# Four output projections as three fp32r products of high and low parts

## What is computed

```
first_block, for each of 2 layers:
    x = x + 0.5 * rms_norm(swiglu(rms_norm(x)))                         # ffn1
    merged = sum over b in conv, nsa, mem of sigmoid(gate_b) * (y_b @ w_branch_b)  # token mixer
    x = x + rms_norm(merged @ w_mix_out)                                # [256,1024] @ [1024,1024]
    x = x + 0.5 * rms_norm(swiglu(rms_norm(x)))                         # ffn2
second_block:
    even layer: concat(ssd scan [256,1024], dilated attention [256,512])
    x = x + concat @ even_w_out                                         # [256,1536] @ [1536,1024]
    odd layer: block attention over 16 heads, gated by silu
    x = x + heads @ odd_w_out                                           # [256,1024] @ [1024,1024]
```

## Time and profile before

| | us |
|---|---|
| median of 3 runs | 1951.61 |
| lowest, highest | 1950.76, 1953.88 |
| profiled execution | 1953.57 |
| its span | 1951.8 |
| PE busy | 1837.4 (94%) |
| DVE busy | 1038.3 (53%) |
| ACT busy | 912.4 (47%) |
| POOL busy | 228.2 (12%) |

### The profile page before, as it was taken

One profiled execution on the slowest core, in us unless ns is written; L12 is line 12 of the kernel. 1 busy time (PEld: TensorE's weight loads), 2 busy tenths in 40 slices (PEclk: granted clock), 3 DMA queues, 4 the chain that ended last, 5 costly groups with the idle time before them and its releaser, 6 DMA issues. The chain is left out here.

```text
span 1951.8 us, 29977 instructions
## 1 busy us (share of the span) xinstructions
PE 1837.4 (94%) x11744; PEld 1576.7 (81%) x11744; DVE 1038.3 (53%) x1976; ACT 912.4 (47%) x1397; POOL 228.2 (12%) x115
## 2 busy tenths in 40 slices
PE   6999999989999989999999989899979899998989
PEld 6999798878599979999897877799969777764875
DVE  7555462346355556554552354555557783552762
ACT  5444433884343444443435882444365444332463
POOL 1000001536200010000004544100010000001000
PEclk9999999999999989999999999999989889799999
DMA  7445456324354444445445323554435333103521
GB/s 286 176 183 193 172 194 245 144 98 159 143 184 176 189 172 160 175 182 194 173 176 236 140 98 136 199 194 177 180 127 194 130 129 130 65 1 129 193 98 55
DMA packets 29900, 311.58 MB, mean 160 GB/s; under 512 B 3312, under 2 KB 3696, under 8 KB 4848
## 3 DMA queue, kind: packets, MB, share of 16 engines
q1 hardware_dynamic: 28944, 307.16, 42.3%
q0 software_dynamic: 864, 3.15, 0.5%
HBM read 309.24 MB, written 1.05 MB: 159 GB/s over the span
## 5 line engine op out<-in xcount | busy, mean ns | idle before, releaser
L428 ACT ACTIVATE region_r<-ring 128x1024 fp32r<-128x1024 f32 x451 | 471.6, 1054 | 422.4 <-PE psum L778 361.5
L778 PE MATMUL psum<-hH,region_r 128*128 128x256 f32 x2240 | 557.0, 287 | 21.5 <-DVE small L2072 8.7
L434 DVE TENSOR_TENSOR ring_r<-ring,region_r 128x1024 fp32r<-128x1024 f32 x398 | 474.8, 1222 | 183.9 <-ACT region_r L428 168.5
L778 PE MATMUL psum<-xs_r,region_r 128*128 128x256 f32 x2240 | 550.6, 284 | 0.0
L778 PEld LDWEIGHTS psum<-hH,region_r 128*128 128x128 f32 x2240 | 425.4, 190 | 36.7 <-DVE small L2072 12.7
L778 PEld LDWEIGHTS psum<-xs_r,region_r 128*128 128x128 f32 x2240 | 425.4, 190 | 4.8 <-issue 0.5
L778 PE MATMUL psum<-hH,ring_r 128*128 128x256 f32 x2336 | 324.7, 281 | 0.0
L778 PEld LDWEIGHTS psum<-hH,ring_r 128*128 128x128 f32 x2336 | 298.3, 189 | 0.0
L434 POOL TENSOR_TENSOR ring_r<-ring,region_r 128x1024 fp32r<-128x1024 f32 x53 | 116.9, 2216 | 1071.2 <-ACT region_r L428 1071.2
L778 PE MATMUL psum<-region_r 128*128 128x512 f32 x704 | 235.0, 395 | 2.1 <-DVE region_r L2019 2.1
L778 PE MATMUL psum<-region_r,hH 128*128 128x512 f32 (+3 forms) x544 | 178.3, 363 | 18.1 <-DVE xs_r L440 6.2
(11 more groups left out here) (213 smaller groups left out, 1895.2 us busy)
## 6 DMA issues: line engine op xcount, KB each, us to landing
ring<-in_weights SPq DMA_DIRECT2D x192, 1536.0 KB, 6.4
gpost<-in_posts POOLq DMA_DIRECT2D x6, 512.0 KB, 5.0
cst<-in_const SPq DMA_DIRECT2D x1, 1198.0 KB, 23.1
xs<-in_mem SPq DMA_DIRECT2D x1, 1024.0 KB, 5.5
x<-in_x SPq DMA_DIRECT2D x1, 1024.0 KB, 7.6
out<-x SPq DMA_DIRECT2D x2, 512.0 KB, 2.6
pars<-in_par SPq DMA_DIRECT2D x1, 368.0 KB, 8.0
p<-in_par SPq DMA_DIRECT2D x1, 206.0 KB, 24.3
```

The source lines that it names most:

```text
L428: eng.activation(unit.high, unit.raw, ACT.Copy).then_inc(h_ready, 1)
L434: eng.tensor_tensor(unit.low, unit.raw, unit.high.bitcast(F32), ALU.subtract).then_inc(l_ready, 1)
L778: ins = pe.matmul(bank, lhsT, rhs, start=start, stop=stop)
```

## The change

The weights of the four projections become split units too: U_OUT (8 in each layer), U_EO (12), U_OO (8). They get places of their own for the high parts (buffers that stand empty in that stage), and `held_before` names the unit after which such a place is empty. The inputs of the projections get high parts (ACT) and low parts (DVE): the merged input in three groups of tiles, the states by half token tile, the heads and head pairs one by one. PE waits for a unit's `l_ready` and for the input's low part, and makes `products` in place of `mm`. SP's list of instructions is the same, POOL's but for one wait.

Where the new instructions stand:

- Mixed. ACT makes OUT highs 0 to 2 with those of the branches, 3 to 7 behind the last branch tile. DVE makes OUT lows 0 to 2 before the branch tiles (6,1), (6,2) and (7,0), the low of the merged tiles 0 to 3 before (7,1), the rest behind the branch stage. POOL starts the lows of FFN2 after the last OUT low. The norm on PE stands between rows 5 and 6.
- Even. The order of the k tiles is 8, 9, 10, 0 to 7, 11 (EO_ORDER; the weights are packed so). The states of token tile 0 are turned, then come three rows, then the states of tile 1, then the other rows. ACT makes EO highs 0 and 1 behind the exponentials of decay steps 6 and 7, 2 to 6 in the attention steps 1 to 5, 7 and 8 in steps 8 and 9, the rest behind it; DVE makes lows 0 and 1 in decay steps 6 and 7, 2 to 6 in steps 6 to 10, the rest behind.
- Odd. ACT makes the eight OO highs in steps 4 to 8 (1, 2, 2, 2 and 1), DVE the lows two at a time in steps 5 to 8. Each collected head pair gets its high on ACT and its low on DVE in later steps. PE does rows 0 and 1 of token tile 1 before rows 6 and 7 of tile 0.

The diff, cut to its core:

```diff
@@ units, places and orders
+OUT_UNITS = [*range(U_OUT, U_OUT + N_OUT)]
+LAYER_SPLIT = [*range(U_FFN1, U_FFN1 + N_FFN), *AB_UNITS, *GATE_UNITS, *BRANCH_UNITS, *OUT_UNITS,
+               *range(U_FFN2, U_FFN2 + N_FFN)]
+EO_ORDER = [8, 9, 10, *range(8), 11]
+MERGED_GROUPS = [(0, 4), (4, 6), (6, 8)]
...
@@ pool
+                        pool.wait_ge(l_ready, Split(U_FFN2).count - 1)
                         lows(range(U_FFN2, U_FFN2 + AHEAD_2))
...
@@ tensor
+                mixed_rows(0, range(KD))
+                mixed_rows(1, range(0, 6))
+                norm(("ffn", 1), k + 1, [0])
+                mixed_rows(1, range(6, KD))
...
+                for n in some:
+                    unit = Split(first + n)
                     if i == 0:
-                        before(kk)
+                        before(n)
+                        pe.wait_ge(l_ready, unit.count)
+                    lhs = parts(n)
...
-                        mm(job.bank, lhs[:, kk, i * P:(i + 1) * P], w[:, c:c + 512],
-                           kk == 0, kk == k - 1, job.full if kk == k - 1 else None)
...
+                        products(job.bank, [h[:, i * P:(i + 1) * P] for h in lhs],
+                                 [w[:, half * 512:(half + 1) * 512] for w in (unit.high, unit.low)],
+                                 n == 0, n == k - 1, job.full if n == k - 1 else None)
...
+            states_turned(0)
+            even_rows(0, range(3))
+            states_turned(1)
+            even_rows(0, range(3, 12))
...
+            odd_rows(1, range(0, 2))
             odd_rows(0, range(6, 8))
-            odd_rows(1, range(8))
+            odd_rows(1, range(2, 8))
@@ scalar
                 act_.activation(e, e, ACT.Exp).then_inc(decay_exp, 1)
+                if n >= 6:
+                    high_part(act_, U_EO + n - 6)
...
+            odd_out_at = {4: (0,), 5: (1, 2), 6: (3, 4), 7: (5, 6), 8: (7,)}
...
+                for n in odd_out_at.get(s, ()):
+                    high_part(act_, U_OO + n)
+                if s >= 4:
+                    mixed_high(s - 4)
@@ vector
+                out_lows = {(6, 1): 0, (6, 2): 1, (7, 0): 2}
...
                     lows_to(EVEN_AT["eb", 10, 0] + n + 3)
+                    if n >= 6:
+                        low_part(dve, U_EO + n - 6)
...
+                if 5 <= s <= 8:
+                    for n in (2 * s - 10, 2 * s - 9):
+                        low_part(dve, U_OO + n)
+                if s >= 5:
+                    mixed_low(s - 5)
```

More of the change, by code:

```diff
@@ L140, in place, with held_before @@
             return kind, (u - first) % PLACES
-    return "ring", u % HIGHS
+    if U_OUT <= u < U_OUT + N_OUT:
+        return "out", u - U_OUT
+    if U_EO <= u < U_EO + N_EO:
+        return ("ring", u - U_EO - 4) if 4 <= u - U_EO < 7 else ("even_out", u - U_EO)
+    if U_OO <= u < U_OO + N_OO:
+        return ("ring", u - U_OO - 2) if u - U_OO >= 4 else ("odd_out", u - U_OO)
+    return "ring", u % HIGHS
+def held_before(u):
+    kind, at = place(u)
+    if kind == "out":
+        return GATE_UNITS[-1] if at < 3 else BRANCH_UNITS[-1]
+    if kind == "even_out":
+        return U_EVEN if at < 2 else U_EVEN + N_EVEN - 1
+    if kind == "odd_out":
+        return U_OB + N_OB - 1
+    return None
 def occupants(units, before):
@@ L150, in occupants @@
         if place(u) not in last:
-            last[place(u)] = units.index(u - place(u)[1]) - 1
+            held = held_before(u)
+            last[place(u)] = units.index(u - place(u)[1]) - 1 if held is None else units.index(held)
         free_at.append(last[place(u)] + 1)
@@ L420, in __init__ @@
                 kind, at = place(u)
-                self.high = {"ring": highs, "gate": gate_highs, "branch": branch_highs}[kind][at]
+                self.high = {"ring": highs, "gate": gate_highs, "branch": branch_highs, "out": out_highs,
+                             "even_out": even_highs, "odd_out": odd_highs}[kind][at]
         def high_part(eng, u, it=0):
@@ L526, in build @@
         at_h = r1.at
-        mt = r1.take(2, SEQ)
+        mt = PcT
         s1 = Space(Sflat, 2304)
@@ L1876, in y_root @@
                         .then_inc(y_std, 1)
-            attention("dil", EVEN_UNITS, y_root)
+                    high_part(act_, U_EO + 7)
+                if s == 9:
+                    high_part(act_, U_EO + 8)
+                    mixed_high(8)
+                    mixed_high(9)
+            attention("dil", EVEN_UNITS, even_highs_made)
+            mixed_high(10)
+            for n in range(4):
+                i, half = n // 2, n % 2
+                Job("yT", n).wait_emptied(act_)
+                some = slice(4 * half, 4 * half + 4)
+                act_.activation(evenH[:, some, i * P:(i + 1) * P], even_mixedT[:, some, i * P:(i + 1) * P], ACT.Copy)\
+                    .then_inc(eH_ready, 1)
+                if n < 3:
+                    high_part(act_, U_EO + 9 + n)
+            mixed_high(11)
             table(ACT.Sqrt)
@@ L1912, in _ @@
             attention("moba", ODD_UNITS, out_gates)
+            for p in range(5, KD):
+                mixed_high(p)
         @block.vector
@@ L2266, in mixer @@
                                 own.settle()
+                merged_low(1)
+                for u in OUT_UNITS[3:5]:
+                    low_part(dve, u)
+                dve.wait_ge(merged, KD * lay[0] + KD)
+                merged_low(2)
+                for u in OUT_UNITS[5:]:
+                    low_part(dve, u)
                 for i in range(NT):
@@ L2728, in tail_chunks @@
     rows = groups([pieces[name] for name in EVEN_ORDER], 3)
-    rows += groups([v["even_w_out_2"][0][k * P:(k + 1) * P] for k in range(12)], 3)
+    rows += groups([v["even_w_out_2"][0][k * P:(k + 1) * P] for k in EO_ORDER], 3)
     rows += groups(blocks(o, [c * 512 for c in range(6)]), 6)
```

177 lines of the change are left out of this document (135 added, 42 removed).

## The result

The changed kernel took 1939.66 us as the median of four runs (1939.53 to 1942.81), the kernel before 1952.48 in four runs beside it. The ratio is 0.9939, with a 95% interval of 0.9921 to 0.9956: faster by 0.6%. The forecast was 1936.0 in a range of 1928 to 1946. The profiled execution took 1939.64 us, its span is 1937.8 where it was 1951.8: 14.0 us less, against 15.6 in the forecast's sum.

A forecast was written before the change was run, and what follows sets the result against it. PE, busy 94% of the span, bounds the kernel. Terms of -9.0 (mixed), -7.9 (even) and +1.3 (odd) sum to -15.6 us: span 1936.2, execution 1938.0, median 1936.0 after taking off 1.96; range 1928 to 1946 for 8 in 10.

The forecast's parts named there:

- PE's saving (24.5): All four projections: three products of 0.231 us replace each 0.863 us matmul; 144 matmuls give 24.5 us.
- Mixed (-4.5 each): Mixed projection, each layer: 5.4 us saved, against 0.7 from late branch tiles and 0.2 with wait and rounding.
- DVE's add: Residual add in the norm after the mixed projection: about 1.1 us longer beside POOL's lows, about 0.1 of PE wait.
- Even (-7.9): Even layer: products -8.2, earlier rows -1.9, later decay +2.2 us.
- The decay: Even layer's last decay step: DVE's low waits for ACT's high, so PE is released 2.2 us later.
- -1.9: Even projection: rows start at 1745.1 instead of 1747.54, with 0.55 us added for turns now among them.
- rival C: Behind the decay's wait: low granted clock held three more steps, about 6 us, giving 1942; chance 0.10.
- Odd (+1.3): Odd layer: 6.6 us of new waits in the attention steps against 5.4 saved, so nothing gained.
- The 1.7 for the low of pair 3: Odd layer: the low of head pair 3 comes at 1928.0, 1.7 us more of wait.
- the 0.6 in the steps ahead: Odd attention: 0.6 us of the 6.6 us of waits, in the steps ahead.
- Rival B: Attention steps: each high-to-low handshake lengthens the path 2.2 us, 33 in all, about 1960; chance 0.07 together with D.
- Rival A: Odd layer: all splits hidden too, taking 6.6 us off, 1929.4; chance 0.17.

The follow-up runs named there:

- the first experiment on the order: Changed kernel with DVE making each low part of the odd layer's output weights a step later, ACT unchanged: 1938.24 us, ratio 0.9922.
- f1: The changed kernel, unaltered, run again as base for the runs beside it: 1941.24 us, ratio 0.9935.
- e1: Changed kernel with DVE's lows of the odd output weights each a step later, the first experiment on the order: 1938.24 us, ratio 0.9922.
- e2: Changed kernel with DVE's first two lows of the even output weights out of the decay steps, all lows moved on two places: 1939.28 us, ratio 0.9927.
- e3: Changed kernel with the odd layer's output projection put back to fp32 matmuls, the other three staying split: 1940.26 us, ratio 0.9930.
- g1: Changed kernel with f2's late odd highs and lows, head pairs ahead of weights on ACT and DVE, step 8's highs before the last copies: 1935.22 us, 0.9902.
- f2: Changed kernel with ACT's odd weight highs at step ends, none in step 5, and DVE using only highs of an earlier step: 1940.56 us, ratio 0.9928.
- e4: Changed kernel with the mixed projections of both layers put back to fp32 matmuls: 1946.61 us, ratio 0.9963.
- h2: Changed kernel with 22 more products of 128x512 ahead of each mixed projection, their result overwritten: 1948.20 us, ratio 0.9966.
- f3: Changed kernel with POOL holding the third branch-weight low until DVE's last low of the branch inputs is made: 1935.16 us, ratio 0.9903.

## Why the prediction was right, step by step

- **PE's saving (24.5).** Right. In the even layer PE went from the first product to the norm's turns in 34.3 us (1739.23 to 1773.57), 0.85 of them turns of states that now lie between; before in 41.3. That is 7.8 for the products, against 8.2.
- **Mixed (-4.5 each).** Right, and term by term. The last branch tiles ended 0.8 us late in both layers (0.7). DVE's add took 2.18 and 1.88 us in place of 1.23, 0.95 and 0.65 more where I had 1.1, and PE's turns of that tile came without a wait in both layers. These are the rows that answer to the earlier trace rows:

```profile
1201.82 2.96 ACT L458 ACTIVATE region_r<-ring 128x1024 fp32r<-128x1024 f32 x3 [1.14 <-DMA ring<-in_weights]
...
1203.12 7.12 POOL L464 TENSOR_TENSOR ring_r<-ring,region_r 128x1024 fp32r<-128x1024 f32 x3 [17.05 <-DVE ring_r L464]
...
1209.45 1.88 DVE L2098 TENSOR_TENSOR x<-x,xs 128x1024 f32<-128x1024 f32 x1
...
1214.30 1.03 PE L838 MATMUL psum<-cst,xs 128*128 128x128 f32 x8
```

  ACT's idle time before FFN2's highs shrank from 19.28 to 1.14 us, as the eight highs fill it; POOL's lows run from 1203.12 to 1210.24, into the add, and PE turns the tile at 1214.30 without a wait. POOL's idle time there ended with DVE's last low: its new wait was the last to end, at 1203, when the first high had been ready for a few tenths. I had put it at nothing, and it cost PE nothing. The add began 0.8 us before POOL's last low ended and became 0.65 longer; in the first layer it began 1.1 before and became 0.95 longer. So it was held to the end of the low that ran, and no whole low, since it began late in one. The Trainium skill's rule ("SBUF — State Buffer", section "Who interferes with whom"), by which such a DVE instruction and one of POOL's exclude each other, agrees with this and with the 3.11 and 0.99 us above: two lows of 128x256 with both inputs in SBUF, beside POOL's lows and free of them.
- **Even (-7.9).** Right at -7.5, but by luck: one term missed by 1.0, and a gain of 1.0 that the sum did not have made up for it. The decay cost 2.1 (2.2), with PE's wait at 3.83 us instead of 2.00. The rows started 1.7 us earlier against the attention, and the turns among them cost 0.85: -0.9 where I had -1.9. The missing 0.7 of the 2.4 lies just ahead of the turns, in the value products of the last two heads. Before, the second head's started in the midst of the first's, at 1741.92; now they start behind them, at 1736.31, and the 24 products take 0.85 us longer, with no wait to see. What they wait for is ACT's last copy of probabilities, which ended at 1736.17: a weight's high and two highs of heads stand ahead of it (1734.13 to 1735.79). PE before, PE now, and that copy:

```profile
1740.56 3.52 PE L778 MATMUL psum<-PTs,region 128*64 128x256 f32 x24
...
1734.08 4.37 PE L831 MATMUL psum<-PTs,region 128*64 128x256 f32 x24
...
1735.69 0.48 ACT L1659 ACTIVATE PTs<-psum 128x384 f32<-128x384 f32 x1
```

  Against it, the full clock came back sooner in the program, which gave 1.0 that the sum did not have (the twelve products of the earlier trace rows took 3.23 us in place of 4.10). The low stretch itself was as long as before, 30.7 us; rival C, a longer one, did not come about.
- **Odd (+1.3).** Right at +1.5, and with the working: ACT's exponential late behind two highs, DVE's wait of 3.17 (2.9), PE's of 3.07 (3.3) and 0.97 (1.0). The 1.7 for the low of pair 3 and the 0.6 in the steps ahead are not in PE's waits: the new ones are 4.0 us, not 6.6. In their place the granted clock fell behind the wait of 3.07: the turning there took 0.97 us instead of 0.82, the values' product behind it 1.56 instead of 0.88, and with the rows behind them it is the 1.6 us of the first experiment on the order. That this makes up for the terms that did not come is luck; some 1.3 us of the loss stand in neither.
- **What the sum had not.** Two terms outside the change: +2.9 in the second layer's branch stage, from the clock, and -1.0 from the first layer's FFN2 on, where the low stretch of the clock behind the norm was 3.4 us in this trace and 6.8 before. The second trace of this kernel (f1) has 3.4 too, but e1, e2 and e3, which are the same program up to there, have 6.8, so it is no effect to count on. With -0.5 ahead of the first stage and small rests these make +1.2; the four stages' deviations, -0.1, -0.1, +0.4 and +0.2, make the other 0.4 of the 1.6 that the span misses on the forecast. I had named a longer low clock as a rival, at the decay; a low stretch came instead in a stage that I had taken as only shifted. The -1.0 hid a third of it.
- **From span to median.** I took off 1.96 us, by which the profiled execution of before lay above its median. The changed kernel's profiled execution lies on its median (1939.64 and 1939.66), so there was nothing to take off: the 1.96 was scatter of the runs. That is the other 2 us between 1936.0 and 1939.66.
- **Rival B** (each handshake on the path) did not happen: two units out of fifteen (3 and 7 of the odd layer) stopped the path, by a step's order. **Rival A** (all hidden) is what g1 nearly reaches, with other order.

## What to carry to other kernels

Where two engines hand a part to each other inside a loop whose steps are chains over both, let the second use only what the first made well before, and put ahead of the waiting part whatever the third engine needs sooner. A hand-over within the step made a gain of 5.4 us into a loss of 1.5 here, the fall of the clock behind the wait included. An earlier step alone gained nothing (f2); with the head pairs ahead as well, the same work kept 4.0 (g1). Look in the trace for engine pairs that slow each other just where a third waits for one of them; there a wait that holds one back gained more than it cost. And count a stage as merely shifted only with a reserve, 3 us here, where a wait of PE stands in it. Last, a sum that comes out is not yet a sum whose terms came out: read each stage's terms too.

## What the runs showed of the hardware beyond that

- A wait of 1.94 to 2.00 us on PE was followed by 3.4 us at granted clock 0.50 in six kernels (seven traces), in the second layer's branch stage, and by 1.00 there in three others (the kernel before, e4 and h2), with the same instructions around it; in the first layer's branch stage it never was. The stage came 4 to 6 us earlier in the six than in the kernel before. Shifting it back, by fp32 matmuls or by added products, took the fall away; what decides between the two was not found.
- The same shows in the odd attention. The wait of 3.06 to 3.08 us ahead of the last turning was followed by 3.4 us at 0.50 in five traces with the odd layer's order of the changed kernel (its own two, e4, f3 and h2), and by 1.00 in e2, which has that order and that wait.
- In the changed kernel's trace, 31 subtractions and additions on DVE with both inputs in SBUF began while a subtraction of POOL's ran. Each took longer than the shortest of its form by the rest of POOL's instruction, less 0.13 to 0.15 us (the 128x256 ones 0.42 us alone and up to 2.54). The 21 gate multiplications that began so, with one input from PSUM, took 0.41 to 0.43 us as the others did. What the meeting costs POOL does not show: its lows of 128x1024 took 1.99 to 2.80 us without such a neighbour, too.
